# A two-block transformer kernel on one Trainium2 core: the second block's output projection as seven half-size products

## The reference, cut to what matters

```python
# block 1 of 2
y = concat([y_att, y_conv, y_pool])           # 512 x 2048
x = layer_norm(ALPHA * x + y @ w_out, ln_g, ln_b)
# block 2 of 2
y = concat([attention_heads, state_space])    # 512 x 2048
x = layer_norm(ALPHA * x + y @ w_out_2, ln_g_2, ln_b_2)
```

## Time and profile before

| | |
|---|---|
| median of 3 runs | 1692.14 us (1691.88 to 1692.17) |
| profiled execution | 1692.62 us |
| its span, first to last instruction | 1690.9 us |
| TensorE's mean granted clock | 0.998 of full speed |
| HBM read, written | 205.93 MB, 25.25 MB |

### The profile page before, as it was taken

The page is one execution under the profiler, slowest core; times in us unless marked ns, Lnnn a source line. Parts: engine busy times, 40 slices in busy tenths (PEclk is TensorE's granted clock), DMA queues, the critical chain, the costliest instruction groups (busy, mean ns, idle before and its releaser), DMA issues.

```text
span 1690.9 us, 21775 instructions
## 1 busy us (share of the span) xinstructions
PE 1677.5 (99%) x7902; PEld 1376.8 (81%) x7902; DVE 914.2 (54%) x1373; ACT 665.4 (39%) x917; POOL 716.4 (42%) x304
## 2 busy tenths in 40 slices
PE   9999999999999999999999999999999999999997
PEld 6888888888888888888888888887668888888886
DVE  6323312332455654988642754748789745556326
ACT  6434434443222225446642333424453545462220
POOL 4433343433444443446554434334235333326551
PEclk9999999999999999999999999999999999999999
DMA  6333233332577844765554342433123222217422
GB/s 238 114 93 92 89 93 94 93 94 82 202 289 292 296 150 139 244 229 185 172 172 156 92 134 87 137 105 119 61 77 100 75 87 75 87 50 275 135 89 100
DMA packets 67360, 232.31 MB, mean 137 GB/s; under 512 B 7336, under 2 KB 7592, under 8 KB 66000
## 3 DMA queue, kind: packets, MB, share of 16 engines
q1 hardware_dynamic: 59184, 206.33, 37.5%
q10 hardware_dynamic: 8096, 24.88, 4.1%
HBM read 205.93 MB, written 25.25 MB: 137 GB/s over the span
## 4 chain that ended last, share of the span: by engine, by line
PE 99%; DVE 1%; DMA 0%; issue 0%; SPq 0%; ACT 0%; DVEq 0%; ACTq 0%
PE bank L575 96%; PE bank L579 2%; DVE feats L1568 0%; DMA feats<-in_x_t 0%; DVE bank L1948 0%; DVE stats L1906 0%; DVE planes_lo L1579 0%; DVE planes_lo L1955 0%; ACT planes_hi L1105 0%; SPq L399 0%; SPq L401 0%; DVE mv L1935 0%; DVE rstd L1924 0%; DVEq L1933 0%; DVEq L1945 0%
## 5 line engine op out<-in xcount | busy, mean ns | idle before, releaser
L525 POOL TENSOR_TENSOR w_lo<-raw,w_hi 128x1024 fp32r<-128x1024 f32 x280 | 693.0, 2480 | 934.8 <-ACT w_hi L1060 934.8
L575 PE MATMUL bank<-planes_hi,w_hi 128*128 128x512 f32 (+1 forms) x1776 | 694.7, 391 | 1.1 <-ACT planes_hi L1105 0.7
L575 PE MATMUL bank<-planes_hi,w_lo 128*128 128x512 f32 (+1 forms) x1776 | 685.3, 386 | 0.0
L575 PE MATMUL bank<-planes_lo,w_hi 128*128 128x512 f32 (+1 forms) x1776 | 684.7, 386 | 0.1
L1060 ACT ACTIVATE w_hi<-raw 128x1024 fp32r<-128x1024 f32 x302 | 320.5, 1061 | 866.4 <-PE bank L575 813.0
L575 PEld LDWEIGHTS bank<-planes_hi,w_hi 128*128 128x128 f32 x1776 | 333.7, 188 | 84.2 <-issue 17.2
L575 PEld LDWEIGHTS bank<-planes_hi,w_lo 128*128 128x128 f32 x1776 | 333.6, 188 | 67.9
L575 PEld LDWEIGHTS bank<-planes_lo,w_hi 128*128 128x128 f32 x1776 | 333.9, 188 | 66.9 <-DVE planes_lo L1579 1.3
L575 PE MATMUL bank<-w_hi,planes_hi 128*128 128x512 f32 x368 | 143.7, 390 | 0.0
L575 PE MATMUL bank<-w_hi,planes_lo 128*128 128x512 f32 x368 | 143.3, 389 | 0.0
L575 PE MATMUL bank<-w_lo,planes_hi 128*128 128x512 f32 x368 | 143.2, 389 | 0.0
(11 more groups left out here) (336 smaller groups left out, 1630.1 us busy)
## 6 DMA issues: line engine op xcount, KB each, us to landing
raw<-in_stream SPq DMA_DIRECT2D x273, 512.0 KB, 3.6
raw<-sums_dram SPq DMA_DIRECT2D x32, 512.0 KB, 4.0
bias<-in_stream SPq DMA_DIRECT2D x10, 512.0 KB, 4.9
probs<-in_stream SPq DMA_DIRECT2D x10, 512.0 KB, 6.9
sums_dram<-bias SPq DMA_DIRECT2D x10, 512.0 KB, 5.2
sums_dram<-probs SPq DMA_DIRECT2D x10, 512.0 KB, 6.7
h_rows<-feats ACTq DMA_DIRECT2D x4, 1024.0 KB, 7.1
feats<-in_x_t SPq DMA_DIRECT2D x7, 512.0 KB, 8.9
```

The source lines that it names most:

```text
L525: nc.gpsimd.tensor_sub(w_lo[:, s, :], raw[:, s, :], w_hi[:, s, :].bitcast(fp32)).then_inc(lo_ready, count)
L575: return nc.tensor.matmul(o, a, b, start=start, stop=stop, skip_group_check=onto)
```

## The change

Block 1's output projection becomes seven half-size products too (`project_sevens2`): rows, inner dimension and columns are cut in halves, and fourteen half products of four units (`HALVES2`: A11, S3, S2, S4, S1, A22, A12, each for two column pairs) replace the four column blocks. A unit now serves two row blocks instead of four: 12 products of 512 columns, 56 units, 672 products. The stage has 28 tiles of two units (`T_END = T_BACK2 + 28`). GpSimd makes the low parts of all 56 units (`SPLIT2` is empty).

What else moves or is new:

- **Sums of weights.** Four sums for each half unit, in 16 rounds: SyncE loads four pieces of 128 x 512 into `wide`, VectorE makes four sums in place (`sum_round`), SyncE stores them to `sums2_dram`. Two rounds lie in each head of block 0 (one after its softmax, one before its finish), and the loads and stores stand between the raw loads on SyncE.
- **Sums of planes.** S3's sum is one VectorE operation after head 1 of block 1; S2, S4 and S1 are summed (VectorE), rounded (ScalarE, `cut_sum2`) and cut (VectorE, `low_sum2`) in the stage itself.
- **gamma and beta of block 0's norm.** ScalarE loads halves of them into `wide` (`load_affine`), VectorE applies them in place to the plain rows (`make_resid`, 16 operations of 1024) after `conv_tile(1)` and `conv_tile(3)`, and ScalarE stores the finished x to `h_rows` (`store_resid`) in place of `store_z`. `finish_resid` is gone.
- **The last head's turn.** The planes are cut in another order (`SECOND_SLOTS`, state-space features first; six instead of four before the last softmax); `head_turn` stands behind unit 3, `head_pv` behind unit 7. ScalarE rounds units 4 to 6 between the exponentials and the probabilities.
- **Taking the half products** (`read_second`): each goes by an addition or a copy into a part of the residual; `fold` adds ALPHA times x for the rows 0 and 1 once it has been loaded. Statistics are taken as each part of a row is final.
- **The end.** The last half product runs row block by row block. Rows 0 and 1 are normed before the reads of half product 12, row 2 after the first row block of the last, row 3 last. SyncE stores rows 0 and 1, ScalarE rows 2 and 3.

The diff, cut to its core:

```diff
-T_END = T_BACK2 + 16
+T_END = T_BACK2 + 28
...
+HALVES2 = [(of, pair) for of in ["A11", "S3", "S2", "S4", "S1", "A22", "A12"] for pair in range(2)]
+SET2_OF = [0, 1, 2, 3, 0, 1, 0, 1, 2, 3, 0, 1, 2, 3]
+STREAMED2 = {"A11": 0, "A12": 16, "S4": 24}
+SPLIT2 = []
+SECOND_HALF_AT = 2
+CUT2 = ["S2 0:4", "S2 4:8", "S4 0:4", "S4 4:8", "S1 0:4", "S1 4:8"]
+SUMMED2 = ["S3", "S2 0:4", "S2 4:8", "S4", "S1"]
 LEFT, RIGHT = slice(S // 2, S), slice(0, S // 2)
...
+            def sum_round(t):
+
+                dve.wait_ge(second_loaded, 64 * (t + 1))
+                b11, b12, b21, b22 = (wide[:, S * i:S * i + S] for i in range(4))
+                step(V.tensor_sub(b22, b22, b12))
+                step(V.tensor_sub(b12, b12, b11))
+                step(V.tensor_add(b11, b11, b22))
+                signal(V.tensor_sub(b21, b21, b11), second_made, t + 1)
...
+            def load_with_round(m, unit, k, t):
+                load_next(m, 0)
+                load_round(unit, k, t)
+                for s in range(1, 4):
+                    load_next(m, s)
+                store_round(unit, k, t)
...
+            def project_sevens2(after_unit):
+
+                for h, (of, pair) in enumerate(HALVES2):
+                    if h == 1:
+                        pe.wait_ge(feat_done, 31)
+                    if h == 3:
+                        pe.wait_ge(feat_done, 32)
+                    if h >= 4:
+                        before = max(g for g in range(h) if SET2_OF[g] == SET2_OF[h])
+                        pe.wait_ge(parts_taken, 15 + before + 1)
+                    if h == len(HALVES2) - 1:
+                        break
+                    for u in range(4):
+                        n = 4 * h + u
+                        wait_unit2(n)
+                        if of in ("S2", "S4", "S1"):
+                            part = [c for c in CUT2 if c[:2] == of and int(c[3]) < 2 * u + 2][-1]
+                            pe.wait_ge(sums_ready, len(CUT) + CUT2.index(part) + 1)
+                        elif of != "S3":
+                            pe.wait_ge(planes_ready, 48 + 2 * u + 2 if of == "A11" else 64)
...
+                    a = 2 * HEADS - 1
+                    cut_second(EARLY[1], 8)
+                    head_exps(a)
+                    round_range(4, 7)
+                    round_probs(a)
                     act.wait_ge(rows_stored, STORED[0])
-                    load_resid(rows_in, 0)
-                    load_resid(rows_in, 1)
-
-                if blk:
-                    for db in range(4):
-                        cols = slice(S * db, S * db + S)
-                        act.dma_start(gamma1[db][:, :], ln1[0:1, cols].to_broadcast([P, S])).then_inc(ln1_loaded[db], 16)
-                        act.dma_start(beta1[db][:, :], ln1[1:2, cols].to_broadcast([P, S])).then_inc(ln1_loaded[db], 16)
+                    for i in range(2):
+                        act.dma_start(probs[:, 2 * i:2 * i + 2, :], col_blocks(2 + i, 0)).then_inc(resid_loaded[1], 16)
+                    round_back(7)
+                    act.wait_ge(feat_done, 31)
+                    cut_second(8, 12)
+                    round_back(8)
+                    cut_second(12, 15)
+                    round_range(9, 12)
+                    act.wait_ge(feat_done, 32)
+                    cut_second(15, KT)
                     act.dma_start(gamma, ln2[0:1, :].to_broadcast([P, D])).then_inc(ln_loaded, 16)
                     act.dma_start(beta, ln2[1:2, :].to_broadcast([P, D])).then_inc(ln_loaded, 16)
...
+                    root(0)
+                    round_back(52)
+                    root(1)
+                    round_range(53, 56)
+                    root(2)
+                    root(3)
+                    store_rows(2)
+                    store_rows(3)
+
...
+            def load_affine(half):
+
+                for i in range(2):
+                    act.dma_start(wide[:, HALF * i:HALF * i + HALF], ln1[i:i + 1, HALF * half:HALF * half + HALF].to_broadcast([P, HALF]))\
+                        .then_inc(ln1_loaded, 16)
+
+            def store_resid():
+
+                act.wait_ge(resid_made, 2)
+                for r in range(QB):
+                    act.dma_start(h_rows[P * r:P * r + P, :], row(r)).then_inc(rows_stored, 16)
+
...
+                def fold(r):
+
+                    for c in range(2):
+                        part = feats[:, 4 * r + c:4 * r + c + 3:2, :]
+                        step(stt(part, part, ALPHA, bias[:, 2 * r:2 * r + 2, :], MULT, ADD))
...
+                    a = 2 * HEADS - 1
+                    cut_second(8, 15)
+                    second_done(0)
+                    dve.wait_ge(resid_loaded[1], 64)
+                    read_second(0)
+                    head_finish(a, HEADS - 1, 32, T_HEAD2 - SK + 2 * HEADS, B[0])
+                    second_done(1)
+                    read_second(1)
+                    cut_second(15, KT)
+                    sum_planes2("S2 0:4")
+                    sum_planes2("S2 4:8")
+                    low_sum2("S2 0:4")
+                    low_sum2("S2 4:8")
+                    sum_planes2("S4")
+                    sum_planes2("S1")
+                    second_done(2)
+                    read_second(2)
+                    second_done(3)
+                    read_second(3)
+                    low_sum2("S4 0:4")
+                    low_sum2("S4 4:8")
+                    second_done(4)
+                    read_second(4)
+                    second_done(5)
+                    read_second(5)
+                    low_sum2("S1 0:4")
+                    low_sum2("S1 4:8")
+                    dve.wait_ge(resid_loaded[0], 64)
+                    fold(0)
+                    fold(1)
+                    dve.wait_ge(resid_loaded[1], 96)
+                    for h in range(6, 12):
+                        second_done(h)
+                        if h > 6 and 4 * h + 7 in SPLIT2:
+                            split_second(4 * h + 7)
+                        read_second(h)
+                    known2(0)
+                    known2(1)
                     dve.wait_ge(ln_loaded, 32)
-                    for r in range(QB):
-                        row_done(r)
-                        norm_rows(r)
+                    norm_rows(0)
+                    norm_rows(1)
+                    second_done(12)
+                    read_second(12)
+                    dve.wait_ge(rows_summed, 2)
+                    read_second(13, [0], 14)
+                    known2(2)
+                    norm_rows(2)
+                    second_done(13)
+                    read_second(13, [1], 15)
+                    known2(3)
+                    norm_rows(3)
...
+            def make_resid(half):
+
+                dve.wait_ge(ln1_loaded, 32 * (half + 1))
+                dve.wait_ge(rows_turned, 4 * QB)
+                for r in range(QB):
+                    part = half_row(r, half)
+                    step(V.tensor_mul(part, part, wide[:, 0:HALF]))
+                    ins = V.tensor_add(part, part, wide[:, HALF:D])
+                    if r < QB - 1:
+                        step(ins)
+                    else:
+                        signal(ins, resid_made, half + 1)
...
             conv_tile(0)
             take_prepared()
             conv_tile(1)
+            make_resid(0)
             conv_tile(2)
             take_decay()
             conv_tile(3)
+            make_resid(1)
             for it in range(1, GROUPS + 1):
...
             head2(HEADS - 1)
-            cut_back(1, 0, EARLY[1])
+            cut_second(0, 4)
             head_finish(2 * HEADS - 2, HEADS - 2, 23 + HEADS, T_HEAD2 - SK + 2 * HEADS - 2)
             a = 2 * HEADS - 1
-            cut_back(1, EARLY[1], 5)
+            cut_second(4, 6)
             head_softmax(a)
-            cut_back(1, 5, 6)
+            cut_second(6, 8)
             head_scale(a)
-            cut_back(1, 6, 7)
-            cut_back(1, 7, 8)
             low_probs(a, low2)
-            cut_back(1, 8, 9)
-            head_finish(a, HEADS - 1, 32, T_HEAD2 - SK + 2 * HEADS, B[0])
-            cut_back(1, 9, KT)
             back_and_norm(1, T_BACK2)
```

More of the change, by code:

```diff
@@ L465, in _ @@
             pair_tile = T_CONV + 7
-            with sp.Fori(2, pair_tile // 2) as m:
+            with sp.Fori(2, 4) as m:
                 for s in range(4):
                     load_next(m, s)
+            for k in range(2):
+                load_with_round(4 + k, 0, k, k)
+            with sp.Fori(3, pair_tile // 4) as pair_of:
+                for k in range(2):
+                    load_with_round(2 * pair_of + k, pair_of - 2, k, 2 * pair_of + k - 4)
             for tile in range(pair_tile, T_MISC):
@@ L494, in _ @@
                         load_decay(g, 1, EB)
-            with sp.Fori(m0 + 2 + 3 * GROUPS, ROUNDS) as m:
+            with sp.Fori(m0 + 2 + 3 * GROUPS, T_BACK2 // 2) as m:
                 for s in range(4):
                     load_next(m, s, MADE)
```

(64 more changed lines are left out.)

298 lines of the change are left out of this document (154 added, 144 removed).

## The result

The changed kernel takes 1700.0 us (median of five, 1699.8 to 1700.5) against 1692.0 (1691.9 to 1692.2): a ratio of 1.0046, 95% interval 1.0034 to 1.0057. It is 8.0 us **slower**. The forecast was 1695.8, with a range of 1684 to 1702 and slower as the likeliest sign; 1700.0 lies beyond the forecast's own band of 1691 to 1699, in that of rival 3. Its span is 1698.3 us (1690.9 before).

The account below looks back on a forecast made before the run. TensorE, busy 99% of the span, bounds the kernel, if its feeder GpSimd keeps up. -21.8 + 3.9 + 4.8 + 4.5 + 1.6 + 10.7 = +3.7 us, so 1692.1 becomes 1695.8 us; range 1684 to 1702.

Parts of the forecast that it names:

- rival 3: More goes wrong: raw loads late beside stores and gamma, or the residual's store reaching tile 8; +1 to +6, 1697-1702; chance 0.16.
- products: TensorE in block 1's output projection: 768 products become 672, 96 fewer at 0.227 us each, -21.8 us.
- loss from unit 12 to 17: Units 13 to 16: VectorE's sums and low parts of S2, S4, S1 slow GpSimd; +4.5 us, bounds 3 and 5.5.
- end of half product 11 (T): End of product group 12 of 14 on TensorE, where the tail begins: 1651.0, including 14.8 us of pauses.
- hidden parts: Weight sums in block 0's heads and gamma and beta work, in VectorE's idle time: zero; gamma and beta at most 1.5 and 3.
- Head turn: Last head: three of four rescalings on VectorE each wait for a GpSimd low part; transposes end 1518.7, not 1514.7: +3.9 us.
- Unit 12: Waits for the last head's result behind VectorE's cuts, then rounding and low part: 1546.9 against TensorE's 1542.2; +4.8, bounds 2 and 5.5.
- Units 28 to 33: S1's low parts and four folds cost GpSimd 1 us each, less a 4.5 us lead: +1.6, bounds 0 and 2.5.
- The tail: VectorE's reads, statistics and norms after T, with four waits behind GpSimd at units 52 to 55: 40.3 us, to 1691.3; +10.7.
- Rival 1: GpSimd and VectorE taking turns on SBUF costs less at VectorE's rescalings, cuts and norms: faster, about 1684; chance 0.2.
- Rival 2: No contention at all between GpSimd and VectorE: only TensorE's -21.8 and 2.5 in the tail, 1673; chance 0.07.
- half-speed unit: TensorE at 1.2 GHz after a pause near 5 us: a unit takes 5.4 us, 2.7 more, absorbed while GpSimd is slower.

Follow-up runs that it names:

- mirror run: Changed kernel with GpSimd's low parts in full, but most VectorE cuts, sums, folds and low parts in block 1's output projection on an eighth of their columns: 1686.5 us.
- seven-unit version: Changed kernel with rescalings before units 4 to 6, last head's result behind three cuts, rows in four loads, VectorE making low parts of 13, 15, 35, 52-55: 1685.7 us.

## Why the prediction was right, and where it was short

The sign, the mechanism and most sizes held. The time came out 4.2 us above the forecast, and 3.5 of them lie in one term. So the range held only because rival 3 had widened it. By the prediction's steps (the loss of a stretch is what it took beyond 2.72 us a unit):

| step | forecast | measured |
|---|---|---|
| products | -21.8 | -21.8 (without GpSimd's work) |
| transposes of the last head end | 1518.7 | 1518.9 |
| unit 12 starts | 1546.9 | 1546.7 |
| loss from unit 12 to 17 | 4.5 | 5.1 |
| unit 17 starts | 1565.0 | 1565.4 |
| loss from unit 17 to 33 | 1.6 (0 to 2.5) | 5.1 |
| end of half product 11 (T) | 1651.0 | 1655.2 |
| from T to VectorE's end | 40.3 | 40.3 |
| hidden parts | 0 | 0 |

**Head turn.** The three rescalings took 2.4, 2.2 and 2.3 us, as worked out. The race that was lost by 0.1 us was lost on the chip too (issued at 1510.39, GpSimd's operation at 1510.26).

**Unit 12.** Right in place and mechanism. Two errors cancelled in its start: the last head's result came at 1540.9 instead of 1540.0, and gamma's and beta's issue cost 0.9 instead of 2.0 us. TensorE reached the unit at 1543.4 instead of 1542.2, mostly by a slower clock (below), so its pause was 3.3 us and not 4.8.

**Units 28 to 33: the mis-sized term.** The first products of units 17, 25 and 33:

```profile
1565.40 0.50 PE L612 MATMUL bank<-w_hi,sum_hi 128*128 128x512 f32 x1 [1.33 <-POOL w_lo L570]
...
1589.24 0.50 PE L612 MATMUL bank<-w_hi,planes_hi 128*128 128x512 f32 x1 [1.25 <-POOL w_lo L570]
...
1614.06 0.50 PE L612 MATMUL bank<-w_hi,sum_hi 128*128 128x512 f32 x1 [0.30 <-POOL w_lo L570]
```

The working gave GpSimd a lead of 4.5 us by unit 28. It had about 1.6 at unit 25: its low part would have been done near 1586.2 had it not stood still for 3.0 us, and TensorE was free at 1587.8. The late load turned that lead into a pause of 1.4 us; with 0.7 lost in tenths from unit 17 on, that makes 2.1. From there to unit 33, with no lead left, TensorE lost 3.0 more, where 1.6 were forecast for all. The prediction took the landing of raw loads as 3.6 us in the whole stage and put "raw loads that land late" into rival 3, with a price of 1 to 6 us and a chance of 0.16. It did not ask when the 2 MB of rows are issued and who loads at that time. With these loads cut up, the stretch lost 1.4 us, close to the forecast, and the kernel won 2.7.

**The tail.** Four waits of 2.0 us stood where they were forecast, and the two last pauses of TensorE, 0.6 and 1.8 us, were the 2.3 of the working. The parts of the tail as written add up to 40.6, not 40.3, so the agreement to a tenth is chance; that to half a microsecond is not.

**The rivals.** Rival 1 (the port costs less) is out: all four places lost their races. Rival 2 is what the kernel does without most of GpSimd's work: it named 1673, the run gave 1673.6. Rival 3 was part of the truth, on top of the forecast and not in its place: its band, 1697 to 1702, is where the time fell, by late raw loads, though beside the residual's rows and not beside the stores and gamma that it names. Its half-speed unit was priced at 2.7 us by doubling 2.72; with 0.43 us a product it would be 2.4.

The sentence from the Trainium skill on the speeds of the two engines held (1.22 against 2.40 us for the same low part), but it was not the reason: the mirror run shows GpSimd keeping up from unit 12 to 51 when most of VectorE's work in SBUF is left out.

## What to carry to other kernels

When a change makes a unit of work shorter on the bounding engine, go through all that is paid once for each unit: here the low part stayed at 2.4 us while its cover fell from 5.4 to 2.72, and wherever GpSimd had no lead left, VectorE's operations on SBUF cost TensorE time. Spread such work, order it by who waits for it, and give some units to the faster engine: that turned 8 us lost into 8.5 us won with the same products. And place each large transfer on the time line of the small ones that feed the bound; cutting it in four was worth 2.7 us.

## What the runs showed of the hardware

**The clock after short pauses.** TensorE's pauses of 1.6 and 2.0 us at the turn, with four transposes between them, were followed by a lower granted clock. Windows of the changed kernel, then of the run with the last head's result first, then of the one with the rescalings first, where only one pause of 1.3 us is left:

```profile
1510.00:1520.00 10.00, 6.50 (x30) 0.88 0.47 156
1520.00:1530.00 10.00, 10.00 (x44) 0.95 0.50 161
```

```profile
1510.00:1520.00 10.00, 6.48 (x29) 0.85 0.44 144
1520.00:1530.00 10.00, 10.00 (x37) 0.80 0.52 174
```

```profile
1510.00:1520.00 10.00, 8.68 (x44) 1.00 0.28 83
1520.00:1530.00 10.00, 10.00 (x49) 1.00 0.80 292
```

At the lower level, 1.2 GHz, products start every 0.43 us instead of 0.227: five of them in the changed kernel, eleven in the second of these runs (1.2 and 2.3 us lost, with a first product that took 0.57). The prediction had expected this only from a pause near 5 us.

Which pause is followed by it differs from run to run. The pause of 3.3 us at unit 12 of the changed kernel was followed by none; one of 2.7 us at the same unit was, in the run with the last four low parts on VectorE:

```profile
1546.00:1550.00 4.00, 3.03 (x13) 1.00 0.86 347
```

```profile
1546.00:1550.00 4.00, 3.88 (x10) 0.57 0.69 278
```

The pause of 4.2 us with the rescalings first was followed by seven such products, which cost nothing since the next units waited for GpSimd anyway; the one of 2.3 us at unit 24 of the seven-unit version by eight. The Trainium skill ("TensorE: Matmul & The Clock Gate", What's actually happening) has the clock fall in an idle array. The rows agree in part: in this stage it fell only around pauses, but not every pause brought it. What decides, and why the same two pauses at the turn cost 1.2 us in one kernel and 2.3 in another, stays open.

**The turns are strict.** In the stretches shown, a VectorE operation on SBUF that had to wait for nearly all of one of GpSimd's took 1.8 to 2.2 us more than alone, whatever its length (0.35 became 2.43, 1.29 became 3.3), and none got ahead of a GpSimd operation that had begun. One kind is spared although its operands lie in SBUF, the statistics, here inside a low part of the changed kernel's tail:

```profile
1656.38 2.40 POOL L570 TENSOR_TENSOR w_lo<-raw,w_hi 128x1024 fp32r<-128x1024 f32 x1 [0.32 <-ACT w_hi L1116]
...
1657.43 0.69 DVE L2082 BATCH_NORM_STATS2 stats<-feats 128x6 f32<-128x512 f32 x1
```
